# Two attention stages in another order: DSA by half chunks and alternating units, MLA by head groups

## The reference, cut to what matters

```python
def dsa_mixer(x, cos, sin, w_in, w_o):
    q, k, v, iq, ik, iw = jnp.split(x @ w_in, A_SPLITS, axis=-1)   # 1024, 256, 256, 512, 64, 8 columns
    # rotary on q, k, iq, ik
    s = jnp.einsum('bqhd,bsd->bqhs', iq_b, ik) * IDX_DIM ** -0.5
    score = jnp.where(causal, jnp.einsum('bqh,bqhs->bqs', iw_b, relu(s)), -inf)
    _, sel = lax.top_k(score, 64)
    # softmax of q k^T over the selected keys, times v: 16 heads of 64, 4 of k and v
    return out @ w_o

def mla_mixer(x, cos, sin, w_dqkv, q_norm, kv_norm, w_uq, w_ukv, w_o):
    down = x @ w_dqkv                       # 256 + 256 latents, 64 rotary key columns
    c_q, c_kv = rms_norm(down[..., :256], q_norm), rms_norm(down[..., 256:512], kv_norm)
    q = c_q @ w_uq                          # 8 heads of 128 + 64 (rotary)
    k_nope, v = split(c_kv @ w_ukv)         # 8 heads of 128 + 128
    # causal softmax of (q_nope k_nope^T + q_rope k_rope^T), times v
    return o @ w_o
```

## Time and profile before

| | us |
|---|---|
| median of 3 executions (1393.74 to 1394.95) | 1394.24 |
| the profiled execution | 1395.76 |
| its span, first to last instruction | 1394.0 |
| PE busy in it | 1309.3 |
| VectorE, ScalarE, GpSimd busy | 831.2, 603.3, 82.6 |
| moved by DMA | 221.07 MB, 159 GB/s |

### The profile page before, as it was taken

One profiled execution on the slowest core, in us unless ns is written; L12 is line 12 of the kernel. 1 busy time (PEld: TensorE's weight loads), 2 busy tenths in 40 slices (PEclk: granted clock), 3 DMA queues, 4 the chain that ended last, 5 costly groups with the idle time before them and its releaser, 6 DMA issues.

```text
span 1394.0 us, 19253 instructions
## 1 busy us (share of the span) xinstructions
PE 1309.3 (94%) x8221; PEld 1183.1 (85%) x8221; DVE 831.2 (60%) x1130; ACT 603.3 (43%) x736; POOL 82.6 (6%) x198
## 2 busy tenths in 40 slices
PE   6978999999998999999878999999999989999998
PEld 5867799998887799998767899998898878999996
DVE  5584765557556755557754744447667657544465
ACT  5453544444723454443442543345552234433334
POOL 2450000000000000000320000000000000000000
PEclk9999999999999999999899999999999999999999
DMA  7410655554732555554421655555543326555542
GB/s 250 151 61 2 211 182 183 188 198 133 223 123 89 183 182 190 196 186 143 152 91 44 218 191 190 182 182 211 169 149 121 121 69 205 179 190 182 181 152 91
DMA packets 128758, 221.07 MB, mean 159 GB/s; under 512 B 6904, under 2 KB 97040, under 8 KB 128672
## 3 DMA queue, kind: packets, MB, share of 16 engines
q1 hardware_dynamic: 125648, 209.83, 44.9%
q0 software_dynamic: 3024, 10.01, 2.5%
HBM read 218.77 MB, written 1.05 MB: 158 GB/s over the span
## 4 chain that ended last, share of the span: by engine, by line
PE 78%; DVE 11%; ACT 6%; DMA 3%; issue 2%; POOL 0%; SPq 0%; ACTq 0%; DVEq 0%; POOLq 0%
PE ps L481 17%; PE ps L482 17%; PE ps L483 17%; PE ps L504 17%; PE ps L591 3%; DVE wlo L1438 3%; PE ps L782 3%; ACT whi L1051 1%; PE ps L647 1%; ACT rot L1077 1%; DVE y L1482 1%; DVE x L1506 1%; DMA raw<-in_ffn_w_in 1%; PE ps L750 1%; ACT buf L1165 1%
## 5 line engine op out<-in xcount | busy, mean ns | idle before, releaser
L1438 DVE TENSOR_TENSOR wlo<-raw,whi 128x2048 fp32r<-128x2048 f32 (+2 forms) x201 | 454.1, 2265 | 242.6 <-ACT whi L1051 242.4
L1051 ACT ACTIVATE whi<-raw 128x2048 fp32r<-128x2048 f32 (+2 forms) x201 | 377.4, 1885 | 171.2 <-DMA raw<-in_ffn_w_in 40.7
L481 PE MATMUL ps<-xh,whi 128*128 128x256 f32 x1272 | 362.4, 285 | 6.4 <-DVE xl L1860 2.5
L483 PE MATMUL ps<-xl,whi 128*128 128x256 f32 x1272 | 361.6, 284 | 0.0
L482 PE MATMUL ps<-xh,wlo 128*128 128x256 f32 x1272 | 361.6, 284 | 0.0
L481 PEld LDWEIGHTS ps<-xh,whi 128*128 128x128 f32 x1272 | 246.0, 193 | 9.5 <-issue 5.0
L482 PEld LDWEIGHTS ps<-xh,wlo 128*128 128x128 f32 x1272 | 245.9, 193 | 1.6
L483 PEld LDWEIGHTS ps<-xl,whi 128*128 128x128 f32 x1272 | 245.8, 193 | 0.0
L481 PE MATMUL ps<-whi,hh 128*128 128x512 f32 x432 | 169.0, 391 | 0.0
L482 PE MATMUL ps<-whi,hl 128*128 128x512 f32 x432 | 168.6, 390 | 0.0
L483 PE MATMUL ps<-wlo,hh 128*128 128x512 f32 x432 | 168.1, 389 | 0.0
(11 more groups left out here) (293 smaller groups left out, 1220.7 us busy)
## 6 DMA issues: line engine op xcount, KB each, us to landing
raw<-in_ffn_w_in SPq DMA_DIRECT2D x44, 1024.0 KB, 5.1
raw<-in_mlp_w_up SPq DMA_DIRECT2D x32, 1024.0 KB, 5.4
raw<-in_mlp_w_down SPq DMA_DIRECT2D x32, 1024.0 KB, 4.9
raw<-in_ffn_w_down SPq DMA_DIRECT2D x22, 1024.0 KB, 4.9
raw<-in_hgrn_w_in SPq DMA_DIRECT2D x16, 1024.0 KB, 5.3
raw<-in_b_w_in SPq DMA_DIRECT2D x12, 1024.0 KB, 5.3
raw<-in_a_w_in SPq DMA_DIRECT2D x8, 1024.0 KB, 7.1
raw<-in_ple_w_gate SPq DMA_DIRECT2D x8, 1024.0 KB, 5.8
```

Source lines behind the costliest of these rows:

```text
L481: mm(o, a[0], b[0], start=start, stop=False)
L483: return mm(o, a[0], b[1], start=False, stop=stop)
L1051: a.activation(whi[:, slot, 0:w], raw[:, slot, 0:w], ACT.Copy).then_inc(s["hi_done"], 1)
L1438: v.tensor_tensor(wlo[:, slot, 0:w], raw[:, slot, 0:w], whi[:, slot, 0:w].bitcast(F32), ALU.subtract).then_inc(s["lo_done"], 1)
```

## The change

In DSA the index queries come first, as four chunks of 2 x 512 columns (`dsa_iq`). The small chunk is computed with its weights held and all 256 positions streaming, and turned back by PE; keys (`dsa_k`) and, behind the queries, values (`dsa_v`) are chunks of 256 columns. Rotations take both tiles in one instruction. One query chunk stands before the index scores and one before the key transposes. `until(n)`, which is `ahead(n - 3)`, places each rounding and each remainder by hand. Attention units alternate between query tile 0 (logits in bank 0, turned probabilities in bank 1) and tile 1 (logits in 2 and 3, probabilities in 4 and 5). An output tile is written in two halves (`BY_HALF`), and tile 0 is turned ahead of the last value products.

In MLA the rounded latents go to `latT`, which lies where `y` lies. Latents of tile 0 are turned beside the small chunk. The projections alternate between banks 0 to 3 and 4 to 7. The first two attention units, with heads 0 to 3, start ahead of the second key/value chunk. The normalising steps of the latents are rearranged into fewer dependent ones. Sizes of the products of MLA, the number of units, and everything outside the two stages stay.

```diff
-        square_chunks("dsa_kvi", a_in, A_K)
+        for q in range(4):
+            chunk("dsa_iq", rows_of(a_in, 2 * q, 2, A_IQ, 512), 2, 512)
         chunk("dsa_small", rows_of(a_in, 0, KD, A_IK, A_SMALL), KD, A_SMALL)
+        chunk("dsa_k", rows_of(a_in, 0, KD, A_K, FG), KD, FG)
         square_chunks("dsa_q", a_in, A_Q)
+        chunk("dsa_v", rows_of(a_in, 0, KD, A_V, FG), KD, FG)
...
+        def probs_bank(u):
+
+            return 1 if u % 2 == 0 else (4 if u < len(ATT_UNITS) - 1 else 2)
...
+            rotate_both(kvi[:, :, 512:1024].rearrange("p t (h d) -> p t h d", d=A_HD), IDX_HEADS)
+            pool.wait_ge(s["small_out"], 1)
+            rotate_both(ikw[:, :, 0:A_HD].unsqueeze(2), 1)
             for tt in range(TT):
-                rotate(kvi[:, tt, 512:1024].rearrange("p (h d) -> p h d", d=A_HD), IDX_HEADS, cosA, sinA, ROT, tt, rot4)
-                rotate(ikw[:, tt, 0:A_HD].unsqueeze(1), 1, cosA, sinA, ROT, tt, rot4)
-                step(g.tensor_copy(ikdup[:, tt, :, :], ikw[:, tt, 0:A_HD].unsqueeze(1).broadcast_to([P, 2, A_HD])))
-                g.tensor_scalar(ikw[:, tt, A_HD:A_SMALL], ikw[:, tt, A_HD:A_SMALL], float(IDX_HEADS**-0.5), None,
-                                ALU.mult).then_inc(s["index_rotated"], 1)
+                last = g.tensor_copy(ikdup[:, tt, :, :], ikw[:, tt, 0:A_HD].unsqueeze(1).broadcast_to([P, 2, A_HD]))
+            step(last)
+            g.tensor_scalar(ikw[:, :, A_HD:A_SMALL], ikw[:, :, A_HD:A_SMALL], float(IDX_HEADS**-0.5), None, ALU.mult).then_inc(s["index_rotated"], 1)
...
+            for c in range(2):
+                pool.wait_ge(s["qr_out"], 2 * c + 2)
+                rotate_both(qrtok[:, :, 256 * c : 256 * c + 256].rearrange("p t (h d) -> p t h d", d=M_ROPE), 4, "qr_rotated", c + 1)
...
+                if j not in BY_HALF:
+                    turn_tile(j, src, 0)
...
-                        o = ps[:, 2 * (u % 2), P * h : P * h + P] if b == 0 else ps[:, 2 * (u % 2) + h // 2, 256 * (h % 2) : 256 * (h % 2) + 256]
+                        o = ps[:, 0, P * h : P * h + P] if b == 0 else ps[:, 2 + h // 2, 256 * (h % 2) : 256 * (h % 2) + 256]
...
+                    if u == n_units - 1:
+                        turn_tile(T_DSA, y, 0)
...
                 logits(0)
+                before_second()
...
+            for q in range(4):
+                by_rows(first["dsa_iq"] + q, 2, 512, 2 * q, KD, [(tt, slice(0, 512), bank(2 + tt)) for tt in range(TT)])
...
+            for part, (w_part, x_part) in enumerate(((0, xh), (1, xh), (0, xl))):
+                for kk in range(KD):
+                    last = mm(ps[0:A_SMALL, 0, 0:SEQ], w[w_part][:, kk, :], x_part[:, kk, :],
...
+            pe.wait_ge(s["index_rotated"], 1)
+            pe.wait_ge(s["k_act"], 1)
+            pe.wait_ge(s["k_dve"], 1)
...
+            by_rows(first["dsa_q"] + 1, 2, D, 2, KD, wide(0))
...
+            for q in range(2, 4):
+                by_rows(first["dsa_q"] + q, 2, D, 2 * q, KD, wide(0))
+            by_rows(first["dsa_v"], KD, FG, 0, KD, [(tt, slice(0, FG), bank(6 + tt, FG)) for tt in range(TT)])
...
+            turn_latents(0)
+            n = first["mla_down"] + 2
+            take(n)
+            rows(n, KD, M_ROPE, 0, KD, [(0, slice(0, M_ROPE), bank(2, M_ROPE))])
+            w = weights(n, KD, M_ROPE)
+            for part, (x_part, w_part) in enumerate(((xh, 0), (xh, 1), (xl, 0))):
+                for kk in range(KD):
+                    last = mm(bank(3, M_ROPE), x_part[:, kk, P:SEQ], w[w_part][:, kk, :], start=(part == 0 and kk == 0), stop=(part == 2 and kk == KD - 1))
+                if part == 0:
+                    turn_latents(1)
...
+                heads_columns(w, 4 * c, 0)
+                pe.wait_ge(s["kr_out"], TT)
+                heads_rows(w, 4 * c + 2, 0, P + M_ROPE).then_inc(s["w_done"], 1)
...
+            heads_columns(w, 0, 2).then_inc(s["kn_done"], 1)
+            pe.wait_ge(s["qr_out"], 4)
+            pe.wait_ge(s["kr_rotated"], 1)
...
+            turn_query_parts(0)
+            heads_rows(w, 2, 2, 2 * P).then_inc(s["w_done"], 1)
+            pe.wait_ge(s["kn_out"], 2)
             pe.wait_ge(s["krT_done"], 1)
+            pe.wait_ge(s["qrT_done"], 1)
+            logits(0)
+            turn_query_parts(1)
+            pe.wait_ge(s["vM_out"], 2)
+            logits(1)
+            n = first["mla_kv"] + 1
+            take(n)
+            w = [v.rearrange("p k (h d) -> p k h d", h=4) for v in weights(n, 2, D)]
+            pe.wait_ge(s["qrT_done"], 2)
+            heads_columns(w, 4, 2).then_inc(s["kn_done"], 1)
+            heads_rows(w, 6, 2, 2 * P).then_inc(s["w_done"], 1)
+            turn_probs(0)
+            pe.wait_ge(s["m_read"], 1)
             pe.wait_ge(s["kn_out"], 4)
+            logits(2)
+            turn_probs(1)
+            pe.wait_ge(s["m_read"], 2)
+            logits(3)
             pe.wait_ge(s["vM_out"], 4)
-
-            def mla_scores(o, b, h, n):
-                mm(o, qnT[:, h, b * P : b * P + P], knT[:, h, 0:n], start=True, stop=False)
-                return mm(o, qrT[:, h // 2, b * P : b * P + P], krT[:, h % 2, 0:n], start=False, stop=True)
-
-            attention(1, ATT_UNITS[1], mla_scores, lambda kt, h: vM[:, kt, P * h : P * h + P], P)
+            values(0)
+            values(1)
+            turn_probs(2)
+            values(2)
+            pe.wait_ge(s["m_read"], 4)
+            turn_probs(3)
+            turn_tile(T_MLA, y, 0)
+            values(3)
...
                 exps(0)
                 for u in range(n_units):
+                    copies(u)
                     if u + 1 < n_units:
                         exps(u + 1)
-                    copies(u)
+                    if u % 2 == 0:
+                        until(first["dsa_o"] + 1 + u // 2)
...
+            act.wait_ge(s["small_turned"], 1)
+            a.activation(ikw[:, :, :], bank(1, TT * A_SMALL).rearrange("p (t c) -> p t c", t=TT), ACT.Copy).then_inc(s["small_out"], 1)
+            until(first["dsa_q"] + 1)
+            act.wait_ge(s["w_done"], first["dsa_k"] + 1)
+            a.activation(kvi[:, 0, 0:FG], bank(4, FG), ACT.Copy).then_inc(s["k_act"], 1)
...
+            query_parts(0)
+            ahead(first["mla_kv"] + 1)
+            query_parts(1)
+            exps(0)
+            ahead(first["mla_o"])
+            act.wait_ge(s["kn_done"], 2)
+            two_banks(knT, 1, 4, "kn_out")
+            exps(1)
+            first_probs(1)
+            exps(2)
+            exps(3)
+            first_probs(3)
...
+                    if u == n_units - 1:
+                        output(u - 1)
+                    if units[u][0] == 1:
+                        copies(u)
                     if u + 2 < n_units:
                         prepare(u + 2)
-                    if u == n_units // 2 - 1:
-                        output(0, 0)
-                output(1, 0)
+                    if u % 2 == 0:
+                        until(first["dsa_o"] + u // 2)
+                    if u in (3, 4):
+                        output(u - 1)
+                turned(T_DSA, 0)
+                output(n_units - 1)
...
+            until(first["dsa_q"] + 1)
+            dve.wait_ge(s["w_done"], first["dsa_k"] + 1)
+            v.tensor_copy(kvi[:, 1, 0:FG], bank(5, FG)).then_inc(s["k_dve"], 1)
+            until(first["dsa_q"] + 2)
+            dve.wait_ge(s["index_rotated"], 1)
...
+                if r == TOPK // 16:
+                    until(first["dsa_v"])
...
+            latent_scale(0)
+            ahead(first["mla_down"])
+            latent_full(0)
+            latent_scale(1)
+            latent_lo(0)
+            latent_full(1)
+            latent_lo(1)
...
+            probs(0)
+            prepare(2)
+            probs(1)
+            prepare(3)
+            output(0)
+            probs(2)
+            output(1)
+            output(2)
+            probs(3)
+            turned(T_MLA, 0)
+            output(3)
...
+ATT_UNITS = [(b, g) for g in range(A_HEADS // 4) for b in range(TT)]
+MLA_UNITS = [(b, g) for g in range(M_HEADS // 4) for b in range(TT)]
```

473 lines of the change are left out of this document (274 added, 199 removed).

## The result

| | us |
|---|---|
| kernel before, median of 4 | 1394.6 |
| changed kernel, median of 4 (1363.42 to 1365.9) | 1364.91 |
| ratio, 95% interval | 0.978 (0.976 to 0.980) |
| profiled execution, its span | 1364.42, 1362.7 |

What follows compares the result with a forecast made beforehand. TensorE, busy 94% of the span, was taken as the bound, with time to win only where it waits, repeats work or runs at low clock. 9.7 + 3.5 + 17.5 = 30.7 us gave 1363.5 us (median's scale), range 1353 to 1375.

Steps and rivals of the forecast that it cites:

- Part 1: DSA up to the first bias addition: reordered projections and an earlier start gain 9.7 us, bounds 4 and 12.
- the wait: Ahead of turning DSA's index queries: PE idles 4.1 us for VectorE's late key copy, with half clock behind it.
- landing term: Kernel start: the first chunk, 0.5 MB instead of 1 MB, lands up to 2.2 us sooner; 2.2 taken, bound 0.
- The slow beginning: Kernel's first 24 wide products: they again cost 2.2 us more than the usual 5.45 us.
- Part 2: DSA attention, first bias addition to output projection: alternating units and moved copies gain 3.5 us, bounds 0 and 6.
- Part 3: MLA projections and attention: earlier query projection, fewer PE waits and less low clock gain 17.5 us, bounds 13 and 21.
- Nothing is given back: Behind both changed stages: order and loads stay as before, so no gain is lost there, 0 us.
- rival A: VectorE remainders hold GpSimd on the path, three in MLA, one before the index queries: 1371 us, chance 0.10.
- B: DSA gives little because splits just ahead of their use come late, each delaying the next: 1373 us, chance 0.18.
- C: Both stages: all waits are covered and the clock stays up, gaining 38.5 us: 1355 us, chance 0.15.
- D: Attention stages: PE stays at 1.2 GHz, so the kernel is slower, up to 1432 us, chance 0.03.
- E: Both stages keep their length because waits on output halves string units together: 1394 us, chance 0.02.

Runs made afterwards that it cites:

- proj_late: Kernel before with the change's DSA projections and old attentions, output projection's roundings and remainders spread between DSA attention units; span 1391.0 us.
- combo2: Changed kernel with key copies ahead of remainders, unused transposes filling PE's waits, and MLA's remainders one place later; median 1350.72 us, ratio 0.968 to the kernel before.
- fill: Changed kernel with 22 unused transposes on PE ahead of its wait for each layer norm's second tile, at five places; span 1360.2 us.

## Why the prediction was right, point by point

**Part 1** (9.7 forecast, 8.3 measured). The first product came at 10.87 (10.8), and the wait at its place, by its releaser and at 4.29 us (4.1). The index scores came at 46.75 for 45.6: 0.5 us because VectorE began the two remainders later than walked, 0.7 because the low clock also took the transposes (2.0 us for 1.1), where I had counted it for products alone. Behind them the walk held, first bias 78.04 for 76.7, 1.3 late. The start's landing term of 2.2 us was right for this profile but not fixed: other executions have up to 2.2 us less of it. The slow beginning, taken over at 2.2 us, cost 2.5 (7.93 for 5.45). The walk gave no cause for it, and the profile shows none: its first four products take 2.04 us, half speed, where PEclk reads 1.00.

**Part 2** (3.5 forecast, 4.3 measured, 7.1 by experiment). The attention's length of 38.7 was 37.9, and its one place of low clock (87 to 93 us) cost 1.7 of the 2.5 left for it, which is the difference. The step that failed is the split between parts: I credited the projections with all that came before the first bias addition. In `proj_late` their gain of 8.3 is worth 5.5 behind the old attention, by more waits and more low clock in about equal parts.

**Part 3** (17.5 forecast, 18.3 measured). 1.0 for 1.9 up to the query projection: my walk left out the 1.27 us wait for the second tile's scaled latents and the half clock behind it. Behind it 17.3 for 15.6: PE waits 2.7 us in all for 15.7 before, a gain of 13.0 where I had 13.7, and that stretch ran at half clock only until 674 us, which cost 2.7 us where I had left 3.7. This makes 15.8; the other 1.5 us are less PE busy time at full clock, which the sum did not have and whose cause stays open. New waits were 1.8 us for the rotated queries (1.5) and 0.9 in the last units (0.5). The reason given for the low clock, 64-column products, was wrong: the latents' wait brings it (`combo2` against `fill`).

**Nothing is given back.** Wrong in both terms, -2.0 behind DSA and +2.4 behind MLA, and right in the sum by luck. Loads and order are the same, as the prediction said, but the clock behind an unchanged wait is not.

**The total.** The spans differ by 31.3 us for a forecast of 30.7. The parts missed by -1.4, +0.8, +0.8 and +0.4 us, so the mechanism holds part by part, and that the total came within 1 us is again in part luck. The high bounds 12 + 6 + 21 make 1355, which lies inside the stated range and not 2 us outside it.

**The port.** Held operations cost 1.8 us on the path, where two were in the sum and 5.4 more were rival A's. **Rivals:** A and B needed losses that did not come, apart from the late key copy, which was in the sum; C needed the clock to stay up, which only `combo2` brought; D and E have nothing for them: PE's clock was 0.982 over the whole, for 0.977.
